# Neighbourhood attention by head pairs in a three-block fp32 kernel on Trainium2

## The reference

```
s_win = einsum(q, k of the window) * scale + bias          # masked outside the window
s_ctx = einsum(q, k_ctx) * scale
p = softmax(concat(s_win, s_ctx))                           # over 256 latent + 256 context keys
o = einsum(p_win, v) + einsum(p_ctx, v_ctx)                 # 8 heads of 64
ctx_attention: p = softmax(q_ctx k_ctx * scale); o = p v_ctx   # context queries, 256 keys, first block only
```

## Time and profile before

| | before |
|---|---|
| median of 3 runs | 2866.43 us (2862.65 to 2871.29) |
| the profiled execution | 2870.06 us |
| its span in the trace | 2868.2 us |
| granted TensorE clock, mean | 0.966 of full |
| TensorE, VectorE, ScalarE, GpSimd busy | 89%, 25%, 16%, 6% |
| neighbourhood stage, layer 0 | about 420 to 573 us |
| neighbourhood stage, layer 1 | about 1497 to 1585 us |

### The profile page before, as it was taken

How to read it: one execution, slowest core, us unless ns; L and a number is a source line. 1 busy time by engine, 2 the same in 40 slices (tenths; PEclk the granted TensorE clock), 3 DMA queues, 4 the chain that set the end, 5 groups by cost and what they waited for, 6 DMA issues and landing times.

```text
span 2868.2 us, 30057 instructions
## 1 busy us (share of the span) xinstructions
PE 2541.6 (89%) x12082; PEld 1539.0 (54%) x12082; DVE 729.1 (25%) x1472; ACT 469.5 (16%) x1027; POOL 173.6 (6%) x199
## 2 busy tenths in 40 slices
PE   6998999999897777769999989777776999998998
PEld 2443445544554444435577755343443868885873
DVE  1657343212400000043343230000002223212211
ACT  2120222201110100022122011010001212202320
POOL 0000000000111111110000011111110000000000
PEclk8999999999999999989999989999998999999999
DMA  7336110231999999953521499999995332233441
GB/s 308 147 125 255 59 60 30 77 129 69 368 424 427 426 426 425 412 235 147 234 89 60 177 377 423 426 426 425 426 388 194 145 120 88 103 147 146 151 155 46
DMA packets 59974, 666.37 MB, mean 232 GB/s; under 512 B 12772, under 2 KB 12932, under 8 KB 20704
## 3 DMA queue, kind: packets, MB, share of 16 engines
q1 hardware_dynamic: 44592, 630.48, 54.1%
q0 software_dynamic: 14416, 31.30, 3.0%
q10 hardware_dynamic: 864, 3.15, 0.3%
HBM read 664.81 MB, written 21.02 MB: 239 GB/s over the span
## 4 chain that ended last, share of the span: by engine, by line
PE 59%; DMA 25%; issue 10%; DVE 4%; ACT 1%; SPq 0%; POOL 0%; POOLq 0%; DVEq 0%; ACTq 0%
DMA branches<-in_w_moe 15%; PE act_bank L638 6%; PE act_bank L649 6%; PE act_bank L735 5%; PE act_bank L1089 4%; PE vec_bank L751 4%; DMA xT<-in_w_moe 4%; PE vec_bank L899 4%; PE score_bank L735 4%; PE vec_bank L735 3%; PE vec_bank L996 3%; PE score_bank L986 3%; DMA heads<-in_w_moe 3%; PE vec_bank L986 2%; PE act_bank L1098 2%
## 5 line engine op out<-in xcount | busy, mean ns | idle before, releaser
L649 PE MATMUL act_bank<-xT,ring 128*128 128x512 f32 (+1 forms) x512 | 195.1, 542 | 10.7 <-DMA ring<-in_w_in 10.7
L638 PE MATMUL act_bank<-ring,xT 128*128 128x512 f32 x448 | 199.1, 602 | 3.4 <-ACT xT L1432 3.4
L2259 DVE TENSOR_TENSOR heads<-work,vec_bank 128x256 f32<-128x256 f32 x64 | 26.9, 421 | 539.6 <-PE vec_bank L986 539.6
L735 PE MATMUL act_bank<-xT,ring 128*128 128x256 f32 (+1 forms) x576 | 157.8, 427 | 1.8 <-ACT branches L1380 1.1
L649 PEld LDWEIGHTS act_bank<-xT,ring 128*128 128x128 f32 x512 | 97.6, 191 | 107.4 <-issue 92.6
L986 PE MATMUL score_bank<-ring,branches 128*64 128x256 f32 x1024 | 120.8, 390 | 30.1 <-issue 17.3
L638 PEld LDWEIGHTS act_bank<-ring,xT 128*128 128x128 f32 x448 | 85.4, 194 | 107.3 <-issue 101.7
L996 PE MATMUL vec_bank<-ring,heads 128*64 128x512 f32 x512 | 116.9, 598 | 29.0 <-DMA ring<-in_w_moe 23.9
L986 PE MATMUL vec_bank<-ring,branches 128*64 128x256 f32 x1024 | 117.2, 381 | 27.3 <-DMA ring<-in_w_moe 27.3
L735 PEld LDWEIGHTS act_bank<-xT,ring 128*128 128x128 f32 x576 | 109.2, 190 | 44.1 <-issue 31.1
L1089 PE MATMUL act_bank<-xT,ring 128*128 128x256 f32 x576 | 128.7, 386 | 0.6 <-ACT work L1681 0.6
(11 more groups left out here) (381 smaller groups left out, 3426.2 us busy)
## 6 DMA issues: line engine op xcount, KB each, us to landing
ring<-in_w_moe SPq DMA_DIRECT2D x96, 2048.0 KB, 36.9
ring<-in_w_in SPq DMA_DIRECT2D x31, 2048.0 KB, 8.8
ring<-in_w_merge SPq DMA_DIRECT2D x27, 2048.0 KB, 7.8
ring<-in_w_ada SPq DMA_DIRECT2D x24, 2048.0 KB, 8.3
branches<-in_w_moe SPq DMA_DIRECT2D x24, 2048.0 KB, 36.9
heads<-in_w_moe SPq DMA_DIRECT2D x24, 2048.0 KB, 36.8
xT<-in_w_moe SPq DMA_DIRECT2D x24, 2048.0 KB, 36.9
values<-in_w_moe SPq DMA_DIRECT2D x24, 2048.0 KB, 37.0
```

The costliest lines, as they stand in the source:

```text
L638: mm = pe.matmul(b.t[:, :], xT[:, k, tile * P:(tile + 1) * P], w[:, k * COLS:(k + 1) * COLS], start=(k == 0), stop=(k == KD - 1))
L649: mm = pe.matmul(b.t[:, 0:n], w[:, k * COLS + f * P:k * COLS + (f + 1) * P], xT[:, k, 0:n], start=(k == 0), stop=(k == KD - 1))
L735: mm = pe.matmul(g.t[:, 0:n], merge_tile(l, i, MERGE_TILES * d + k), xs[:, k, 0:n], start=(k == 0), stop=(k == KD - 1))
```

## The change

The stage works on pairs of heads (2f, 2f + 1) of a tile.

- `scores` waits for V[0] and V[1] and issues both heads' products, one in each row half, into one bank each, one pair ahead.
- VectorE's `scored` does the additions and copies of both heads and then both maxima. A new step, `shares`, waits for both exponentials, takes the reciprocal of both sums, and divides the probabilities of each head in place, before TensorE transposes them (`turn`).
- `value` takes 64 columns of values as weights and the 128 transposed probabilities as moving data. Head m of the pair writes partitions `64 * m` to `64 * m + 63` of the output bank, so the output is head columns by queries, which is the layout that the merge reads. The two heads alternate.
- Gone are `normed`, the transposes of `o_rows`, and the copies behind them. ScalarE copies each tile's bank into `ysT` directly (`out`), and TensorE waits for the copies of the last two tiles.
- Merge work comes in the same portions, one ahead of `turn` and one ahead of `value`. The loops ahead of a head (`attend`) are not used here any more; values are multiplied in the iteration of their own pair.

```diff
@@ -491,7 +491,7 @@
     rope_done = count("rope_done")
     neg_max_done = count("neg_max_done")
     mix_done = count("mix_done")
...
+    na_exp_done, p_done = count("na_exp_done"), count("p_done")
     o_done = count("o_done")
     merge_done = count("merge_done")
     h_done = count("h_done")
@@ -829,56 +829,64 @@
             count_fills("neighbourhood", l)
 
         def neighbourhood(l):
...
+            pairs = [(tile, f) for tile in range(tiles(l)) for f in range(4)]
+            parts = 2 * len(pairs) // MERGE_UNITS
 
             def scores(i):
...
+                tile, f = pairs[i]
                 kt = key_tiles(tile)
...
+                for m in range(2):
+                    pe.wait_ge(V[m].free, V[m].fills)
+                for m in range(2):
+                    r = 64 * m
+                    pe.matmul(V[m].t[:, 0:len(kt) * P], qcT[r:r + 64, f, tile * P:(tile + 1) * P],
+                              kcT[r:r + 64, f, kt[0] * P:NT * P], start=True, stop=True).then_inc(V[m].full, V[m].fill())
+                    mark["scored", l, i, m] = at_bank(V[m])
+                    mark["s_free", l, i, m] = let_go(V[m])
+
+            def turn(i):
+                tile, f = pairs[i]
+                for m in range(2):
+                    b = A[m]
                     pe.wait_ge(p_done.sem, p_done.take("pe"))
...
+                    pe.wait_ge(b.free, b.fills)
+                    for j in range(len(key_tiles(tile))):
+                        mm = pe.transpose(b.t[:, j * P:(j + 1) * P], probs[:, i % 2, m, j * P:(j + 1) * P], ident)
+                    mm.then_inc(b.full, b.fill())
+                    mark["turned", l, i, m] = at_bank(b)
+                    mark["pT", l, i, m] = let_go(b)
 
             def value(i):
...
+                tile, f = pairs[i]
                 kt = key_tiles(tile)
                 o = V[2 + tile % 2]
...
+                if f == 0:
                     pe.wait_ge(o.free, o.fills)
...
+                for m in range(2):
+                    pe.wait_ge(*mark["pT", l, i, m])
                 for j, k in enumerate(kt):
...
+                    for m in range(2):
+                        c0 = (2 * f + m) * 64
+                        mm = pe.matmul(o.t[64 * m:64 * m + 64, f * P:(f + 1) * P], vc[:, k, c0:c0 + 64], mixT[:, m, j, :],
+                                       start=(j == 0), stop=(j == len(kt) - 1))
+                if f == 3:
                     mm.then_inc(o.full, o.fill())
...
+                    mark["o_full", l, tile], mark["o", l, tile] = at_bank(o), let_go(o)
+
+            scores(0)
+            for i in range(len(pairs)):
+                if i + 1 < len(pairs):
+                    scores(i + 1)
+                merge_between(l, 1, 2 * i, parts, S[0], S[1])
+                turn(i)
+                merge_between(l, 1, 2 * i + 1, parts, S[0], S[1])
+                value(i)
+
+            mark["used", "bias", l, 0] = mark["turned", l, 7, 1]
+            last = tiles(l) - 1
+            mark["attended", l] = mark["o_full", l, last]
+            for tile in (last - 1, last):
                 pe.wait_ge(*mark["o", l, tile])
...
 
         def merge(l, first, xs=xT, ys=ysT):
             count_fills("merge", l)
@@ -1532,32 +1540,44 @@
             resume("neighbourhood", l)
 
         def neighbourhood(l):
...
+            pairs = [(tile, f) for tile in range(tiles(l)) for f in range(4)]
+            parts = 2 * len(pairs) // MERGE_UNITS
 
             def exps(i):
...
+                tile, f = pairs[i]
                 n = n_keys(tile)
...
+                for m in range(2):
+                    q = 2 * (i % 2) + m
+                    if i >= 2:
+                        act.wait_ge(*mark["turned", l, i - 2, m])
+                    act.wait_ge(neg_max_done.sem, neg_max_done.take("act"))
+                    src = mix[:, m, :] if tile < 2 else V[m].t[:, 0:n]
+                    ins = nc.scalar.activation(probs[:, i % 2, m, 0:n], src, ACT.Exp, bias=neg_max[:, q:q + 1],
+                                               accum_out=na_sum[:, i % 2, m:m + 1])
+                    if tile < 2:
+                        ins.then_inc(na_exp_done.sem, na_exp_done.up())
+                    else:
+                        ins.then_inc(V[m].free, 1)
+
+            def out(tile):
+                b = V[2 + tile % 2]
+                act.wait_ge(*mark["o_full", l, tile])
+                nc.scalar.activation(ysT[:, 2, :, tile * P:(tile + 1) * P], b.t[:, :].rearrange("p (a n) -> p a n", a=4),
+                                     ACT.Copy).then_inc(b.free, 1)
 
             exps(0)
...
+            for i in range(len(pairs)):
+                tile, f = pairs[i]
+                if f == 0 and tile >= 1:
+                    out(tile - 1)
+                if i + 1 < len(pairs):
                     exps(i + 1)
...
+                half_tanh_between(l, 1, 2 * i, parts)
+                kt = n_keys(tile) // P
+                for m in range(2):
+                    evacuate(A[m], mixT[:, m, 0:kt, :], n=kt * P, shape=kt)
+                half_tanh_between(l, 1, 2 * i + 1, parts)
+            out(tiles(l) - 1)
 
         def merge(l, first):
             resume("merge", l)
@@ -2044,47 +2064,52 @@
             resume("neighbourhood", l)
 
         def neighbourhood(l):
...
+            pairs = [(tile, f) for tile in range(tiles(l)) for f in range(4)]
+            parts = 2 * len(pairs) // MERGE_UNITS
             bias_slot, bias_turn = AT["bias", l, 0]
             bias = ring[bias_slot][:, 0:4096].rearrange("p (h t n) -> p h t n", h=8, t=2)
...
 
             def scored(i):
...
+                tile, f = pairs[i]
+                q = 2 * (i % 2)
+                for m in range(2):
+                    b = V[m]
+                    dve.wait_ge(*mark["scored", l, i, m])
+                    if tile >= 2:
+                        negmax(neg_max[:, q + m:q + m + 1], b.t[:, 0:CTX])
+                    else:
+                        TT(mix[:, m, 0:SEQ], b.t[:, 0:SEQ], bias[:, 2 * f + m, tile, :], ALU.add)
+                        nc.vector.tensor_copy(mix[:, m, SEQ:], b.t[:, SEQ:]).then_inc(b.free, 1)
+                if tile < 2:
+                    for m in range(2):
+                        dve.wait_ge(*mark["s_free", l, i, m])
+                        negmax(neg_max[:, q + m:q + m + 1], mix[:, m, :])
+
+            def shares(i):
+                tile, f = pairs[i]
+                for m in range(2):
+                    if tile < 2:
+                        dve.wait_ge(na_exp_done.sem, na_exp_done.take("dve"))
+                    else:
+                        dve.wait_ge(*mark["s_free", l, i, m])
+                inv = na_inv[:, i % 2, 0:2]
+                step(nc.vector.reciprocal(inv, na_sum[:, i % 2, 0:2]))
+                for m in range(2):
+                    p = probs[:, i % 2, m, 0:n_keys(tile)]
+                    TS(p, p, inv[:, m:m + 1], None, ALU.mult).then_inc(p_done.sem, p_done.up())
 
             dve.wait_ge(ring_loaded[bias_slot], 16 * (bias_turn + 1))
             for w in mark["da_turned", l]:
                 dve.wait_ge(*w)
...
+            scored(0)
+            shares(0)
+            for i in range(len(pairs)):
+                if i + 1 < len(pairs):
+                    scored(i + 1)
+                    shares(i + 1)
+                d, q = divmod(2 * i + 1, parts)
+                if q == parts - 1:
+                    gated_sum(l, 1, d, gate_1)
 
         def merge(l, first):
             resume("merge", l)
```

More of the change, by code:

```diff
@@ L831, in neighbourhood @@
         def neighbourhood(l):
-            items = [(tile, hd) for tile in range(tiles(l)) for hd in range(8)]
+            pairs = [(tile, f) for tile in range(tiles(l)) for f in range(4)]
+            parts = 2 * len(pairs) // MERGE_UNITS
             def scores(i):
-                tile, hd = items[i]
-                b = V[i % 2]
+                tile, f = pairs[i]
                 kt = key_tiles(tile)
[L838 to L848, removed]
-                    pe.wait_ge(p_done.sem, p_done.take("pe"))
[L850 to L857, removed]
+                for m in range(2):
+                    pe.wait_ge(V[m].free, V[m].fills)
@@ L869, in value @@
-                if hd == 7:
-                    mm.then_inc(o.full, o.fill())
[L871 to L877, removed]
+                    for m in range(2):
+                        c0 = (2 * f + m) * 64
+                        mm = pe.matmul(o.t[64 * m:64 * m + 64, f * P:(f + 1) * P], vc[:, k, c0:c0 + 64], mixT[:, m, j, :],
+                                       start=(j == 0), stop=(j == len(kt) - 1))
@@ L1553, in neighbourhood @@
-            exps(0)
-            for i in range(len(items)):
-                if i + 1 < len(items):
-                    exps(i + 1)
[L1557 to L1560, removed]
+                for m in range(2):
[10 more added lines that the diff above has]
+                        ins.then_inc(V[m].free, 1)
```

26 lines of the change are left out of this document (removed).

## The result

The changed kernel takes 2825.76 us (median of four runs, 2815.75 to 2831.07), the one before 2865.51 beside it: 39.75 us less, a ratio of 0.9861 with a 95% interval of 0.9838 to 0.9884 (33 to 46 us). The forecast was 38 us less.

A forecast was written before the change was run, and what follows sets the result against it. TensorE's instruction stream was taken to bound the neighbourhood stage. Savings of 29.8 + 7.8 - 2.1 (first pairs' scores) - 1.4 (later start) + 4.0 (end) = 38.1 us gave 2828 us from the median 2866.4; range 2820 to 2846.

The forecast's parts named there:

- Scores of a pair: Neighbourhood stage: both heads' score products run side by side in row halves, saving 1.05 us with 512 keys, 0.63 with 256.
- Values of a pair with 512 keys: Value product with 64-column weights in two column halves: 16 instructions at 0.054 us each, 0.86 us.
- The end: End of the stage, last value loads to first merge load: 1.0 us, saving 4.0 us over both layers.
- The later wait for both banks: Start of the stage: the second pair needs both banks, so merge work starts some 0.7 us later, minus 1.4 for two layers.
- Period: TensorE's time for two heads with 512 keys in the stage: 8.3 us in place of 10.2.
- The pairs as a whole: Saving per pair: 1.86 us with 512 keys (16 pairs, 29.8 us), 0.98 with 256 (eight pairs, 7.8 us).
- The drains: TensorE's changes of array shape: three per pair in place of four per two heads, taken as 0.2 us each.
- late warm-up: Start of the stage in both layers: a slow clock start, allowed for as a loss in the forecast's own range to 2837.
- The first rival: Value product: column halves don't share time, by exposed loads or taking turns; 17.2 us less saved, 2845 us; chance 0.08.
- The second rival: Copies of turned probabilities on ScalarE come late and stall 16 pairs by 1 us each; 2844 us; chance 0.13.
- The third: Value bursts drop the granted clock to the 1.2 GHz level; about 2943 us if all layer 0's stage; chance 0.03.
- The fourth: After the stage: something fixed in time, a load, sets the experts' start, so time stays at 2866 us; chance 0.04.

## Why the prediction was right, and where it was off

**The terms of the sum.** Scores of a pair: forecast 1.06 us, measured 1.06, and 1.05 of a head's own is what keeping them apart gave back. Values of a pair with 512 keys: forecast 0.86 and 0.2 of drain, measured 1.03. The end: forecast 1.0 us, measured 0.96 and 0.95. The later wait for both banks: forecast 0.7 us more, measured 1.69 - 0.94 = 0.75. Period: forecast 8.3, measured 8.31. Carried through, 38.1 us stand against two comparisons of medians: 2865.51 - 2825.76 = 39.75 and 2860.78 - 2823.82 = 37.0.

**The pairs as a whole.** A pair with 512 keys saves 10.20 - 8.31 = 1.89 us where I had 1.86, one with 256 keys 1.01 where I had 0.98. Over 24 pairs that is 0.7 us more than forecast.

**The drains.** I took three of 0.2 us, and they do come to 0.6: 8.31 less 0.86 for values, 0.85 for scores, 5.12 for the merge and 0.86 for transposes leaves 0.62. They are divided otherwise than I said. Leaving the column halves costs 0.17 and the way from row halves to full 0.2. From the first merge load to the values' first it is 469.92 - 463.70 = 6.22 us, 0.24 over merge and transposes. Only some 0.09 of that stands at the entry into column halves: the last merge load is at 460.67, its matmul starts 0.43 later and takes 0.43, and the values' first load is at 461.61. Most of the rest is the first merge load, which no matmul covers; six merge matmuls take 2.68 us from the first to the transposes behind them (424.36 - 421.68), not 2.56. I had put that part into the 0.18 ahead of the scores. So the sum was right, its parts were not, and that they came to 0.6 is partly luck.

**The clock.** The two stages show 42.9 us less in the traces where I had 38.1. Of the 4.8 us between, 4.3 are the full clock that the first profile of the changed kernel had at the start of layer 0's stage; a wait of 0.42 us ahead of the first values there, which I had not summed, takes some of it back; the pairs give 0.7. The second profile of the same program has the lower level there, and its two stages show 40.8 us less. I had allowed for a late warm-up in the range, as a loss. The profile that I summed against had it already, so against that profile the clock could only help. Whoever sums against one profiled execution should ask which of its stretches ran at the lower level by chance.

**The first rival**, turns instead of overlap, had 0.08. It is wrong as a description of the changed kernel: its values run at 0.054 per instruction. The rule of the Trainium skill that stood beside it ("TensorE: Matmul & The Clock Gate", section "The mechanism") does not hold for this shape: the sixteen loads, all on the same rows, take 0.85 us and run beside the matmuls. I had quoted that rule alone; the same section of the Trainium skill also lets loads into the background weight buffer go ahead, which would fit the trace; no run shows which buffer the loads went to. As a price it was wrong too. When I took the alternation away I expected the 17 us of that rival and got 7.4, because TensorE starts some instructions of the free half early.

**The second rival**, the loop through ScalarE, had 0.13, and the sum left 0.5 us to spare in pairs with a tanh. Mechanism right, size off: it is 1.0 us there and 1.5 without a tanh. The copies end 468.88 - 462.64 = 6.24 us behind the issue of the scores where I had 6.7, and TensorE asks for them at 7.28 where I had 7.2. Part of this is VectorE: additions and copies of both heads start 456.83 - 455.49 = 1.34 us ahead of the maxima where I had 1.6. Four added copies cost what the larger slack says.

**The third**, the clock as a lasting loss, did not show: in the granted clock of a stretch inside the stage (columns as in rows 2) nothing fell. Its price was mixed up in the prediction: the gain is gone once 38 us of full-speed work run at the lower level, which then take 76 us. The 122 us that I set beside the 76 were full-speed work.

```profile
440.00:460.00 20.00, 20.00 (x95) 10.32 (x94) 10.91 (x26) 8.46 (x20) 0.00 (x0) 1.00 0.00 0
```

VectorE is busy for 10.9 of 20 us in place of 7.2 and ScalarE for 8.5 in place of 5.8, and TensorE for all of it: they stay hidden.

**The fourth**, that the gain is given back later, did not show either: the stretch between the stages, which holds the experts of layer 0, lasts 922.4 us against 923.8, and what lies behind layer 1's stage 1281.9 against 1283.5.

## What to carry to other kernels

Two products that use half of the array's rows, or half of its columns, are worth issuing side by side, and the orientation of a product can be chosen to make them so: compare weight columns with moving columns, since here the longer of the two set the pace (128 of weights with 64 moving: 0.107 us; 64 of weights with 128 moving, in two alternating halves: 0.054). Alternate the halves instruction by instruction, or in short blocks. Once TensorE's stream gets shorter, look at what has a fixed length beside it: here the start of the stage, where issuing the first pair ahead of another stage's wait gave some 7 us more.

## What was new about the hardware

TensorE works on the other column half ahead of instructions that wait for the busy one: with four of a kind in a row a pair's sixteen instructions take 1.07 us, with eight 1.51, against 1.03 alternating and 1.9 for strict turns. The trace of eight in a row puts the reach at three or four waiting instructions, by estimate; no run varies the block length between four and eight, nor shows whether the reach is the same for row halves. Entering column halves from full-array work cost some 0.09 us, leaving them 0.17.
